# Long attention: probabilities weighed on GpSimd, token tile 0's turned probabilities copied by VectorE

## The reference, cut to what matters

```python
sc = jnp.where(vis, einsum('bgrqd,bgnd->bgrqn', qb, k_cmp), NEG)      # 15 compressed keys
p_cmp = softmax(sc) * any(vis)
o_cmp = einsum('bgrqn,bgnd->bgrqd', p_cmp, v_cmp)
sc = jnp.where(pos <= t, einsum('bgrqd,bgrqk', qb, ksel), NEG)        # selected blocks: all keys
o_slc = einsum('bgrqk,bgqkd->bgrqd', softmax(sc), vsel)
sc = jnp.where(wmask, einsum('bgrqd,bgkd->bgrqk', qb, kwin), NEG)     # window: all keys
o_win = einsum('bgrqk,bgkd->bgrqd', softmax(sc), vwin)
return gb[..., 0:1] * o_cmp + gb[..., 1:2] * o_slc + gb[..., 2:3] * o_win
```

## Time and profile before

| | us |
|---|---|
| median of 3 runs | 1682.86 |
| lowest and highest | 1681.2, 1683.01 |
| span of the profiled execution | 1682.8 |
| TensorE busy in it | 1614.8 |
| VectorE busy | 1041.9 |
| ScalarE busy | 753.0 |
| GpSimd busy | 92.8 |

### The profile page before, as it was taken

How to read it: one execution, slowest core, us unless ns; L and a number is a source line. 1 busy time by engine, 2 the same in 40 slices (tenths; PEclk the granted TensorE clock), 3 DMA queues, 4 the chain that set the end, 5 groups by cost and what they waited for, 6 DMA issues and landing times.

```text
span 1682.8 us, 21776 instructions
## 1 busy us (share of the span) xinstructions
PE 1614.8 (96%) x8397; PEld 1346.4 (80%) x8397; DVE 1041.9 (62%) x1365; ACT 753.0 (45%) x949; POOL 92.8 (6%) x147
## 2 busy tenths in 40 slices
PE   7999998999999999999989999999989999999997
PEld 7888877888888888889975787888778877678886
DVE  5577666576765586755667555555557776775444
ACT  5444443444444344344358454434444455354432
POOL 1000000000100000001000021000010030200000
PEclk9999998999999999999989999999999999999999
DMA  9587744287775587763350343655645531555550
GB/s 336 199 293 252 238 142 177 88 282 263 252 246 178 172 278 262 238 222 120 104 178 1 106 145 133 221 176 198 189 166 200 186 130 51 201 177 197 187 200 26
DMA packets 210489, 311.83 MB, mean 185 GB/s; under 512 B 16569, under 2 KB 145621, under 8 KB 210160
## 3 DMA queue, kind: packets, MB, share of 16 engines
q1 hardware_dynamic: 204400, 288.90, 51.0%
q0 software_dynamic: 6016, 21.94, 3.7%
HBM read 306.59 MB, written 4.21 MB: 185 GB/s over the span
## 4 chain that ended last, share of the span: by engine, by line
PE 85%; DVE 7%; ACT 3%; issue 1%; DMA 1%; DVEq 1%; PEld 1%; POOL 0%; ACTq 0%; PEldq 0%; POOLq 0%
PE ps L2276 25%; PE ps L2278 25%; PE ps L2277 25%; DVE wlo L1445 2%; PE ps L2337 1%; PE ps L2472 1%; ACT whi L791 1%; PE ps L2612 1%; PE ps L2757 1%; DMA area<-in_gate_b 1%; PE ps L2589 1%; DVEq L1409 1%; ACT xn L1134 1%; DVE aT_lo L1478 1%; PE ps L2325 0%
## 5 line engine op out<-in xcount | busy, mean ns | idle before, releaser
L1445 DVE TENSOR_TENSOR wlo<-raw,whi 128x2048 fp32r<-128x2048 f32 x247 | 562.7, 2295 | 215.3 <-ACT whi L791 214.7
L791 ACT ACTIVATE whi<-raw 128x2048 fp32r<-128x2048 f32 x251 | 474.8, 1910 | 169.7 <-PE ps L2278 144.1
L2276 PE MATMUL ps<-wlo,aT_hi 128*128 128x512 f32 (+2 forms) x1296 | 508.5, 392 | 12.2 <-DVE aT_lo L1478 7.2
L2278 PE MATMUL ps<-whi,aT_hi 128*128 128x512 f32 (+2 forms) x1296 | 499.9, 386 | 0.0
L2277 PE MATMUL ps<-whi,aT_lo 128*128 128x512 f32 (+2 forms) x1296 | 499.3, 385 | 0.0
L2276 PEld LDWEIGHTS ps<-wlo,aT_hi 128*128 128x128 f32 x1296 | 245.6, 190 | 64.2 <-issue 12.3
L2278 PEld LDWEIGHTS ps<-whi,aT_hi 128*128 128x128 f32 x1296 | 245.0, 189 | 49.1
L2277 PEld LDWEIGHTS ps<-whi,aT_lo 128*128 128x128 f32 x1296 | 245.8, 190 | 46.3 <-issue 0.5
L2276 PE MATMUL ps<-wlo,hT_hi 128*128 128x512 f32 (+1 forms) x496 | 192.3, 388 | 0.0
L2278 PE MATMUL ps<-whi,hT_hi 128*128 128x512 f32 (+1 forms) x496 | 191.5, 386 | 0.0
L2277 PE MATMUL ps<-whi,hT_lo 128*128 128x512 f32 (+1 forms) x496 | 191.3, 386 | 0.0
(11 more groups left out here) (336 smaller groups left out, 1232.2 us busy)
## 6 DMA issues: line engine op xcount, KB each, us to landing
raw<-in_ffn_w_in SPq DMA_DIRECT2D x176, 512.0 KB, 4.8
raw<-in_ffn_w_out SPq DMA_DIRECT2D x88, 512.0 KB, 4.2
raw<-in_w_ff SPq DMA_DIRECT2D x64, 512.0 KB, 4.7
raw<-in_ada_w SPq DMA_DIRECT2D x48, 512.0 KB, 5.3
raw<-in_w_in SPq DMA_DIRECT2D x48, 512.0 KB, 4.8
raw<-in_xattn_w_kv SPq DMA_DIRECT2D x32, 512.0 KB, 7.2
raw<-in_xattn_w_q SPq DMA_DIRECT2D x16, 512.0 KB, 5.6
raw<-in_xattn_w_o SPq DMA_DIRECT2D x16, 512.0 KB, 6.1
```

Source lines behind the costliest of these rows:

```text
L791: act.activation(to, of, ACT.Copy).then_inc(hi_ready[slot], 1)
L1445: dve.tensor_tensor(lo, of, hi, ALU.subtract).then_inc(lo_ready[slot], 1)
L2276: pe.matmul(o, lh, rl, start=start, stop=False, skip_group_check=True)
L2278: return pe.matmul(o, lh, rh, start=False, stop=stop, skip_group_check=True)
```

## The change

GpSimd gets a loop over the 32 units: it waits for a new semaphore `inverted`, makes the two multiplications in place in `Pb`, and raises `weighed`. VectorE's `weigh` becomes `invert`, which only takes the reciprocals and raises `inverted`; its wait for itself is gone. ScalarE's `keep` returns at once for units of tile 0; VectorE gets a `keep` for these, placed after nsa_top(u+3) for unit u-1. In place of the one counter `probs_kept` there are two, `kept_tile[0]` (raised by VectorE) and `kept_tile[1]` (by ScalarE), and TensorE's waits in `turn` and `values` take the one that fits. At the end of the stage ScalarE waits for the sixteenth copy of VectorE and raises `probs_kept` by 32 at once.

```diff
 # GpSimd, nsa_attend
+for u in range(32):
+    t, b = u // 4 % 2, 2 * (u % 4)
+    w, h = P * (t + 1), 4 * (u // 8) + u % 4
+    pool.wait_ge(inverted, u + 1)
+    for j in range(2):
+        p = Pb[u % 4][:, w * j:w * j + w]
+        last = pool.tensor_scalar(p, p, rec4[:, b + j:b + j + 1], gates[:, t, 3 * h + 1 + j:3 * h + 2 + j],
+                                  ALU.mult, ALU.mult)
+    last.then_inc(weighed, 1)
 # ScalarE, keep(u)
+if t == 0:
+    return
-   .then_inc(probs_kept, 1)
+   .then_inc(kept_tile[1], 1)
 # ScalarE, end of the stage
+act.wait_ge(kept_tile[0], 16)
+act.drain().then_inc(probs_kept, 32)
 # VectorE
-def weigh(u):
+def invert(u):
     dve.wait_ge(exped, units.n + u + 1)
-    step(dve.reciprocal(rec4[:, b:b + 2], den4[:, b:b + 2]))
-    for j in range(2):
-        ... dve.tensor_scalar(p, p, rec4[...], gates[...], ALU.mult, ALU.mult)
-    last.then_inc(weighed, 1)
+    dve.reciprocal(rec4[:, b:b + 2], den4[:, b:b + 2]).then_inc(inverted, 1)
+def keep(u):
+    gi, r = u // 4, u % 4
+    dve.wait_ge(probs_turned, units.n + u + 1)
+    if gi >= 2:
+        dve.wait_ge(pv_done, groups.n + gi - 1)
+    dve.tensor_copy(nsaP[gi % 2][:, r, 0:2 * P], ps[:, 4 + u % 2, 0:2 * P]).then_inc(kept_tile[0], 1)
 for u in range(32):
-    weigh(u)
+    invert(u)
     if u + 3 < 32:
         self.nsa_top(u + 3)
+    if u and (u - 1) // 4 % 2 == 0:
+        keep(u - 1)
 # TensorE
+def kept(u):
+    return 4 * (u // 8) + u % 4 + 1
-pe.wait_ge(probs_kept, U - 1)
+pe.wait_ge(kept_tile[(u - 2) // 4 % 2], kept(u - 2))
-pe.wait_ge(probs_kept, units.n + 4 * gi + 4)
+pe.wait_ge(kept_tile[t], kept(4 * gi + 3))
```

More of the change, by code:

```diff
@@ L155, in build @@
         scored, maxed, exped, weighed = sem("scored"), sem("maxed"), sem("exped"), sem("weighed")
+        inverted = sem("inverted")
+        kept_tile = [sem(f"kept_tile{t}") for t in range(T)]
         probs_turned, probs_kept, pv_done = sem("probs_turned"), sem("probs_kept"), sem("pv_done")
@@ L1903, in nsa_attend @@
                     enter()
-                    def weigh(u):
-                        t, b = u // 4 % 2, 2 * (u % 4)
-                        w, h = P * (t + 1), 4 * (u // 8) + u % 4
+                    def invert(u):
+                        b = 2 * (u % 4)
                         dve.wait_ge(exped, units.n + u + 1)
-                        step(dve.reciprocal(rec4[:, b:b + 2], den4[:, b:b + 2]))
-                        for j in range(2):
-                            p = Pb[u % 4][:, w * j:w * j + w]
-                            last = dve.tensor_scalar(p, p, rec4[:, b + j:b + j + 1], gates[:, t, 3 * h + 1 + j:3 * h + 2 + j],
-                                                     ALU.mult, ALU.mult)
-                        last.then_inc(weighed, 1)
+                        dve.reciprocal(rec4[:, b:b + 2], den4[:, b:b + 2]).then_inc(inverted, 1)
[5 more added lines that the diff above has]
+                        dve.tensor_copy(nsaP[gi % 2][:, r, 0:2 * P], ps[:, 4 + u % 2, 0:2 * P]).then_inc(kept_tile[0], 1)
                     def out_lo(gi):
```

## The result

| | median us | lowest to highest | runs |
|---|---|---|---|
| before | 1677.83 | 1676.41 to 1683.71 | 14 |
| changed | 1685.63 | 1683.21 to 1686.92 | 14 |

What follows compares the result with a forecast made beforehand. The prediction took a loop of waits through several engines, none full, to bound the long attention. Three periods at 0.56 + 0.1 + 0.58 (3.7 us) plus 1.1 at the ends gave +4.9, so 1687.7 us, range 1681.8 to 1696.0.

Steps and rivals of the forecast that it cites:

- The duration p: One GpSimd multiplication of 256 columns, taken as 0.35 us fixed plus 0.25 us for columns, 0.60 us.
- Rivals 1 and 2: GpSimd at two-input rate, 1690 to 1697 us, chance 0.17; or GpSimd quick and the kernel not slower, chance 0.22.
- Segment A: Long attention, ScalarE's out_hi copy to TensorE's turn of unit 15: GpSimd's latency bare, 2.28 against 1.72 us, +0.56.
- Segment B: Long attention, TensorE alone with scores, turns and values, 6.26 us: unit 17 comes late through GpSimd, +0.1 us.
- Segment C: Long attention, turn(18) to tile 0's next out_hi: chain moves from ScalarE to VectorE and GpSimd, 6.68 against 6.10 us, +0.58.
- The prediction's other path: Same stretch before tile 0's out_hi, through top(23), keep(19) and reciprocal(21): longer if a GpSimd multiplication takes below 0.6 us.
- Three periods and the ends: Long attention: three whole periods add 3.7 us, the stage's start and end 1.1 us.
- The walk: The long attention's chain of waits, followed again with the new queues: +4.9 us together.
- The last A: End of the long attention, out_hi at 931.80 to turn(31): GpSimd's latency once more, +0.56 us.
- The first C: Start of the long attention, up to 889.42: the longer VectorE and GpSimd chain once more, +0.58 us.
- rival 4: Granted clock falls in the long attention where TensorE waits longer; at half clock 1694 us; chance 0.04.
- Rival 3: VectorE's tensor reductions in the long attention hold GpSimd up, 5.5 us more, 1693 us; chance 0.05.

Runs made afterwards that it cites:

- out_lo late: VectorE's out_lo subtraction moved behind the next unit's reciprocal in the changed kernel, ratio 1.0017; behind its weighing in the kernel before, ratio 0.9991.
- with zeros in both: Matmuls of zeros put in TensorE's waits, in the changed kernel (ratio 1.0011, 1681.66 us) and in the kernel before (1.0001, 1678.99 us).
- one softmax each: Changed kernel, but GpSimd multiplies only the window softmax, VectorE the selected one, and ScalarE makes all copies: ratio 0.9991, 1678.48 us.

## Why the prediction was right, and where not

- **The duration p.** Taken 0.60, measured 0.545 from start to start: the fixed 0.35 was right to the digit, the column was 0.83 ns and not 1.0. Rivals 1 and 2 lay at the ends of this unknown and both fell. The Trainium skill, GPSIMD Engine Reference, § 3.1, with 1.03 cycles a column, is 0.86 ns at its 1.2 GHz; the trace agrees, with 0.83.
- **Segment A.** +0.56 forecast, +0.43 measured; with p = 0.545 its formula gives +0.45. With out_lo late it falls to 0.56, though 0.77 of that comes back in B.
- **Segment B.** +0.1 forecast, +0.13.
- **Segment C.** +0.58 forecast, +0.27 measured, the term most off, though its path is the one foreseen up to turn(20): top, copy, reciprocal, GpSimd. From there the chain shown goes over ScalarE's copies and exponentials, which end within 0.1 us of the path over unit 21 (turn 913.27, and 2.34 more). Of the 0.31, 0.22 is p (four of them, 2.18 against 2.40), the rest are hops and the stretch behind turn(21). The prediction's other path, over top(23) and keep(19), would by its formula give +0.46 at p = 0.545 and be the longer one; the two came out level, because reciprocal(20) held VectorE up for 0.07 and not 0.16 and the hops were shorter.
- **Three periods and the ends.** The walk gave 3 x 1.24 + 1.1, and a period of 15.1 to 15.5. Measured are 3 x 0.83 = 2.5 from the loop and a period of 14.91, outside that range. The last A (+0.56) is not there: in the changed kernel turn(31) didn't wait for GpSimd, because the zeros ahead of it ran at 1.2 GHz and held TensorE instead (four took 2.08 us, 1.20 in the kernel before). The first C can't be told from the clock. By the prediction's own formulas its forecast range for p, 0.45 to 0.75, is 1685.2 to 1691.3 and not 1684.5 to 1690.5, and p = 0.57 gives 4.3 us and not 4.2; nothing hangs on either.
- **The clock**, rival 4, with a chance of 0.04 and called unlikely because the windows read had 0.97 to 1.00. This is the step that failed. All 14 runs of the changed kernel have a lower granted clock than the median run before (0.984 to 0.986 against 0.990), at an equal clock the two differ by some 1 us, and with zeros in both by 1.7 to 2.7. In the two profiles set side by side some 4.6 of 7.05 us lie in windows of lower clock (the start holds the first C too, so this is an upper bound). So the loop is some 2 to 3 us of the 5.9, by the periods and the kernels with zeros, and the clock the rest, an estimate from these figures. The sum of 4.9 came out near the measured 5.9 by luck: two errors had opposite signs, a loop forecast at twice its size and a clock put at nothing. The first profile of before had shown the clock at 0.66 to 0.84 around the start, and the prediction used only windows from 889 on.
- **Rival 3**, VectorE holding GpSimd up. In the changed kernel it didn't: its 128 columns take 452 ns, and with four instructions a unit 453. What VectorE does there reads one SBUF tensor beside PSUM. Where its multiplication with source and result in SBUF ran beside GpSimd's (one softmax each), 0.07 to 0.14 us were lost in each instruction by the means. By the Trainium skill, SBUF — State Buffer, § Who interferes with whom, this is a kind of VectorE instruction that can take the ports shared with GpSimd, and one with a single SBUF input beside PSUM isn't; the trace agrees, with 0.69 in place of 0.55 us in the first case and 0.56 in the second.

## What to carry to other kernels

In a stage where no engine is full, busy sums say little about a move from one engine to another: ScalarE at 11.9 of 14.08 us was relieved of 0.7 and the period grew by 0.76. Walk the loop instead, and put the slow engine's latency where its consumer has other work in its queue; a wait that stands in front of a ready unit, as out_lo did, was worth as much here (0.83 us a period) as the whole move to the other engines had cost. And where a change adds waits to TensorE, read the granted clock over the whole stage, its start and end too, and in every run: here about half of the price lay in it, an estimate.

## What the runs showed of the hardware

- A multiplication on GpSimd with two per-partition operands costs 0.35 us fixed and 0.83 to 0.86 ns a column of float32 (397, 452 and 558 ns for 64, 128 and 256 columns, the first with four instructions a unit); a second one starts about 0.01 us before the first ends.
- The granted clock of one program differs from run to run in a stage with waits: 73.2 and 68.9 us for the same instructions. Eight matmuls of zeros (2.11 us) in a wait of 3 us, and two ahead of every second turn of an odd pair, brought the changed kernel's granted clock over a whole run to between 0.985 and 0.993, from between 0.984 and 0.986.
- A reciprocal of two columns that nothing waits for on its own engine lets VectorE's next instruction start 0.07 us later, where the walk had 0.16, the duration in its record: 906.55 and 906.62 in the changed kernel's timeline.

```profile
906.22 0.42 DVE L1930 COPY area<-ps 128x256 f32<-128x256 f32 x1
906.55 0.16 DVE L1923 RECIPROCAL small<-small 128x2 f32<-128x2 f32 x1
906.62 0.41 DVE L1893 CUSTOM_DVE_ANT_0 xn<-ps,cst 128x256 f32<-128x256 f32 x1
```
